# Identity products on TensorE between the adaLN dot products of a decoder layer

## The reference

```python
mod = (jax.nn.silu(c) @ w_ada[l] + b_ada[l]).reshape(b, N_MOD, D_MODEL)
sh1, sc1, g1 = mod[:, 0], mod[:, 1], mod[:, 2]
...
h = modulate(x, sh1, sc1)      # LayerNorm(x) * (1 + sc1) + sh1
y = swiglu(h, ffn1_w_gate[l], ffn1_w_up[l], ffn1_w_down[l])
x = layer_norm(ALPHA * x + 0.5 * g1[:, None, :] * y, ln1_g[l], ln1_b[l])
```

## Time and profile before

| | |
|---|---|
| median of the timed runs | 2340.41 us (3 runs, 2339.27 to 2340.97) |
| the profiled execution's own time | 2345.88 us |
| its span on the slowest core (core 5) | 2344.3 us |
| spans of the other cores | 2330.9 to 2340.4 us |
| PE busy on core 5 | 2258.2 us (96%) |
| DVE, ACT, POOL busy on core 5 | 1447.6, 765.0, 389.6 us |

### The profile page before, as it was taken

How to read it: one execution, slowest core, us unless ns; L and a number is a source line. 1 busy time by engine, 2 the same in 40 slices (tenths; PEclk the granted TensorE clock), 3 DMA queues, 4 the chain that set the end, 5 groups by cost and what they waited for, 6 DMA issues and landing times.

```text
span 2344.3 us, 41640 instructions; the slowest of 8 cores (2330.9 to 2344.3 us)
## 1 busy us (share of the span) xinstructions
PE 2258.2 (96%) x13832; PEld 1269.6 (54%) x13832; DVE 1447.6 (62%) x2928; ACT 765.0 (33%) x1554; POOL 389.6 (17%) x319
## 2 busy tenths in 40 slices
PE   1999999999999999999999999999999999999998
PEld 1554555555555556644555555555555555555555
DVE  5464465665564343378767676768585868676754
ACT  2521222222222232344343433434343343433321
POOL 0022321221110110013211111111111121211110
PEclk9899999999999999999999999999999999999999
DMA  9962879976563122043645464636464555554556
GB/s 310 312 226 102 163 196 210 199 189 162 180 211 97 71 80 83 1 171 109 238 175 204 161 218 149 224 145 225 153 215 163 202 177 198 180 191 169 208 183 239
DMA packets 123122, 415.48 MB, mean 177 GB/s; under 512 B 27296, under 2 KB 49568, under 8 KB 101408
## 3 DMA queue, kind: packets, MB, share of 16 engines
q1 hardware_dynamic: 87920, 396.92, 49.9%
q0 software_dynamic: 33696, 14.62, 5.3%
q10 hardware_dynamic: 1296, 1.29, 0.2%
HBM read 385.33 MB, written 56.10 MB: 188 GB/s over the span
## 4 chain that ended last, share of the span: by engine, by line
PE 88%; DVE 4%; DMA 3%; issue 2%; SPq 1%; POOL 1%; ACT 1%; DVEq 0%; POOLq 0%; ACTq 0%
PE ps L497 25%; PE ps L1237 24%; PE ps L1260 13%; PE ps L603 10%; PE ps L1046 3%; PE ps L1016 2%; PE ps L1164 2%; PE ps L1166 2%; PE ps L442 2%; PE ps L578 1%; SPq L367 1%; DMA t_arena<-ffn_w_down 1%; DMA t_arena<-w_ada_t 1%; PE ps L1135 1%; PE ps L1072 1%
## 5 line engine op out<-in xcount | busy, mean ns | idle before, releaser
L497 PE MATMUL ps<-t_arena 128*128 128x384 bf16 x3872 | 643.9, 329 | 20.5 <-ACT t_arena L424 17.3
L1237 PE MATMUL ps<-t_arena 128*128 128x384 bf16 (+1 forms) x3872 | 635.2, 322 | 1.2 <-DVE t_arena L426 1.2
L497 PEld LDWEIGHTS ps<-t_arena 128*128 128x128 bf16 x3872 | 381.2, 99 | 278.8 <-issue 29.4
L1237 PEld LDWEIGHTS ps<-t_arena 128*128 128x128 bf16 x3872 | 372.5, 98 | 243.8 <-issue 20.9
L392 POOL TENSOR_TENSOR t_stt<-t_stt,t_mhalf 128x1 f32<-128x1 f32 x193 | 120.5, 624 | 1436.3 <-DVE t_stt L391 1396.9
L399 ACT ACTIVATE t_arena<-t_arena,t_stt 128x1024 f32<-128x1024 f32 (+1 forms) x193 | 238.9, 1239 | 305.5 <-DVE t_stt L394 288.3
L488 DVE TENSOR_TENSOR t_arena<-ps,t_sg 128x384 bf16<-128x384 f32 x242 | 134.4, 556 | 318.6 <-PE ps L497 298.8
L1260 PE MATMUL ps<-t_arena 128*128 128x512 bf16 x1408 | 314.0, 379 | 1.7 <-DMA t_arena<-scr_d 1.7
L603 PE MATMUL ps<-t_arena 128*128 128x512 bf16 x1320 | 293.5, 382 | 4.7 <-DVE t_arena L550 4.7
L388 DVE BATCH_NORM_STATS2 t_stt<-t_arena 128x6 f32<-128x512 f32 x386 | 266.9, 692 | 41.2 <-DMA t_arena<-x_c 13.1
L527 POOL TENSOR_TENSOR t_arena<-t_arena 128x1024 f32<-128x1024 f32 x95 | 229.1, 2412 | 354.3 <-DVE t_arena L526 341.3
(11 more groups left out here) (90 smaller groups left out, 1524.4 us busy)
## 6 DMA issues: line engine op xcount, KB each, us to landing
t_arena<-scr_gu SPq DMA_DIRECT2D x121, 1024.0 KB, 6.6
t_arena<-scr_d SPq DMA_DIRECT2D x44, 1024.0 KB, 5.8
t_arena<-w_ada_t SPq DMA_DIRECT2D x72, 512.0 KB, 9.3
t_arena<-x_c SPq DMA_DIRECT2D x66, 512.0 KB, 5.4
t_arena<-scr_x SPq DMA_DIRECT2D x65, 512.0 KB, 6.6
t_arena<-ffn_w_gu SPq DMA_DIRECT2D x44, 512.0 KB, 10.8
t_arena<-ffn_w_down SPq DMA_DIRECT2D x44, 512.0 KB, 5.5
scr_x<-t_arena SPq DMA_DIRECT2D x33, 512.0 KB, 3.8
```

Source lines behind the costliest of these rows:

```text
L497: ins = e.matmul(bk.f[:, 0:T], lhsT=w.ap[:, kc, gu, s2 * 128:(s2 + 1) * 128], rhs=hT.ap[:, kc, 0:T], start=(kc == 0), stop=(kc == 7))
L1237: ins = e.matmul(bk.f[:, 0:T], lhsT=wv[:, kc, gu, s2 * 128:(s2 + 1) * 128], rhs=hTc.ap[:, kc, 0:T], start=(kc == 0), stop=(kc == 7))
```

## The change

A new generator `warm` issues n products of the 128 x 128 identity with itself into a PSUM bank of `FB`. It declares that it reads the buffer it is given, here `B_msc[1]`, so that it follows the last operation that wrote it. `ada_first` calls it after dots 9, 11 and 13 (60 products each), and after the last bias (40 products). The products' results are not used. Nothing else is edited; the line numbers behind the new code move by 10 to 14.

```diff
+        def warm(n, after_buf):
+            bk = yield from take(FB)
+
+            def mm(e, bk=bk):
+                for k in range(n):
+                    ins = e.matmul(bk.f[:, 0:128], lhsT=ident[:], rhs=ident[:], start=True, stop=True)
+                return ins
+            yield Op("pe", mm, [after_buf, B_const], [bk.buf], n * 0.06)
+            FB.give(bk)
+
         def ada_first():
             yield from until("csr0")
             for i in range(16):
@@
                 if i % 8 == 7:
                     yield mod_bias(i // 8, i // 8)
                     flags.add(("msc", i // 8))
+                if i in (9, 11, 13):
+                    yield from warm(60, B_msc[1])
+                elif i == 15:
+                    yield from warm(40, B_msc[1])
```

## The result

The changed kernel takes 1.0055 times the time of the kernel before (95% interval 1.0038 to 1.0072, seven runs of each; medians 2355.64 and 2340.83 us). Two of the seven runs of the change and one of the seven of before fell in a slower state of the chip; the ratio leaves them out, the medians count them. On the 2340.41 us of the runs shown that is +12.9 us, interval +8.9 to +16.9, or some 2353.3 us. I had forecast 2346.5 us, +6.1. The direction was right, the forecast size was half of the measured one.

A forecast was written before the change was run, and what follows sets the result against it. PE bounds the kernel behind 320 us, DVE's dots its start. Gate-up 15.8 us later, less give-backs, left +9.9, +7.8, +3.5 us on cores 0, 1, 5; taken as +6.1: 2346.5 us, range 2338 to 2354.

The forecast's parts named there:

- The dots wait: Before gate-up: dots 10, 12, 14 wait for bursts of 5.4, 5.0 and 5.0 us; gate-up starts 15.8 us later.
- The give-backs to the gate row: Up to the gate row: four terms leave +9.9, +7.8 and +3.5 us on cores 0, 1 and 5.
- the 1.0 us of clock that I left it: Behind the second tile's transposes: low clock after the new wait still costs 1.0 us.
- The new wait behind the transposes: After the second tile's transposes: PE idles 2.0 us for their evacuation, replacing the wait of about 3 us before them.
- It stays the shorter, so the 24 products that were moved are hidden in waits that PE had there: Gate row to down products: PE's 41.3 us stays below the multiplications' 44 to 46; uncovered, 24 products cost 3.9 us.
- last condition: Sign of being wrong: the stretch after the gate row takes up more than 3 us of the delay.
- The median's shift: Whole kernel: the median run moves by +6.1 us, to 2346.5 us.
- The last step, from three cores to the slowest of eight: End of the sum: between core 1 and core 5, the median's slowest core shifts 6.5 us, taken as 6.1.
- Only the first burst is cold: Rival, chance 0.24: the clock holds through the pauses, bursts take 11.9 us together, time 2342 us.
- Identity products don't raise the clock: Rival, chance 0.12: all bursts take 6.5 us, gate-up starts cold as before, time some 2354 us.
- Faster: Rival, chance 0.09: core 5's lost clock sets the time; short bursts and a shorter gate-row stretch give 2335 us.
- Refills of weights: Later weight loads: SP's refills wait some 10 us longer for casts but cost nothing; no gate-up product waits.

The follow-up runs named there:

- e1: The changed kernel with the same 220 products, but the bursts not declared as readers of the dots' buffer, so no dot waits: ratio 1.0003 to the kernel before.
- e2: The changed kernel with the bursts' estimated duration set to zero, giving the order of before while the dots' waits stay: ratio 1.0050 to the kernel before.
- e3: The changed kernel's order and waits, but each burst is one product instead of 60 or 40: ratio 1.0005 to the kernel before.
- e8: The changed kernel with its order kept and 120 products instead of 60 in the three bursts that dots wait for: ratio 1.0102 to the kernel before.
- e5: The changed kernel with its order kept and 30 products instead of 60 in the three bursts that dots wait for: ratio 1.0047 to the kernel before.
- e6: The changed kernel's order with no identity products and no waits for PE, made by longer estimated dots: ratio 0.9998 to the kernel before.
- e10: The changed kernel's order with no dot waiting, and e4's bursts of 60 and 16 products: ratio 0.9991 to the kernel before.
- e4: The changed kernel with no dot waiting and only 60 products after dot 13 and 16 after the bias: ratio 1.0006 to the kernel before.
- e7: e4 plus 36 identity products that wait for nothing, in PE's pause ahead of the second tile's transposes: ratio 0.9986 to the kernel before.
- e9: The kernel before plus only 36 identity products in PE's pause ahead of the second tile's transposes: ratio 1.0000 to the kernel before.
- e11: e7 run again on another chip: ratio 0.9971 to the kernel before.

## Why the prediction was right and where it was wrong

**The dots wait: right.** The bursts took 5.9, 4.8 and 4.0 us on the mean of the cores, 14.7 together, where I had 5.4, 5.0 and 5.0. Gate-up started 14.8 us later, where I had 15.8. The clock rose in the bursts, and fell in half of the pauses: of the sixteen bursts behind one, eight took 4.8 to 5.4 us, six took 3.51, and the third on cores 0 and 1 took 4.10 at a granted clock of 0.81. e1 and e2 show that the waits and not the products cost the time, e3 and e8 that the cost follows the bursts' length; e5 lies between them by its start, and nearer to the change than expected by its time.

**The give-backs to the gate row: right on the mean, wrong by core.** Of 14.8 us 7.6 were left at the gate row on the mean of eight; my three cores had 9.9, 7.8 and 3.5, a mean of 7.1. That the means agree is in part luck. Core 5 had +1.0 for my +3.5: its gate-up started 14.4 us later and not 15.8, and it didn't lose the 1.0 us of clock that I left it. Cores 0 and 1 had +15.7 and +13.7 for my +9.9 and +7.8, with a clock of 0.81 for a while, which I had not among my terms. The new wait behind the transposes was 1.9 to 2.2 us, predicted 2.0.

**"It stays the shorter, so the 24 products that were moved are hidden in waits that PE had there": this step failed.** I set the stretch behind the gate row at its old length and noted that uncovered the 24 products would cost 3.9 us. It grew from 43.7 to 46.8 us, 3.1 of these 3.9. I had set PE's path at 41.3 us of products, without the waits inside, and had read the room for them from core 5.

The waits have to be told apart. The last one, ahead of L578, was 2.5 us on the mean before (1.12 to 4.50) and is 1.0 us now, and 1.0 us stays even where the L488 waits only for PE. So 1.4 us of room was there, not 3.9. Core 5 had the most, and there the step held: its stretch went from 46.4 to 45.7 us. Cores 0 and 1 had shown a last wait of 1.12 us in my own rows, and grew by 2.1 and 2.7 us. The waits inside the stretch, for L488s that free PE's banks, grew from 2.4 to 3.6 us. Where PE waits there, the L488 stands behind pairs of multiplications on DVE. On core 5 of the changed kernel, DVE, then PE:

```profile
150.36 4.50 DVE L746 TENSOR_TENSOR t_arena<-t_arena 128x1024 bf16<-128x1024 f32 x2
154.78 1.01 DVE L488 TENSOR_TENSOR t_arena<-ps,t_sg 128x384 bf16<-128x384 f32 x2
```

```profile
155.47 20.96 PE L497 MATMUL ps<-t_arena 128*128 128x384 bf16 x128 [1.84 <-DVE t_arena L488]
```

With PE's busy time up by 3.4 us (38.8 to 42.2), these make the 3.1: +3.4, -1.4, +1.2, but for rounding. In the runs with the new order (e3, e5, e6, e8, e10) the stretch is 46.1 to 47.4 us and in those with the old order (e1, e2, e4, e7, e9, e11) 42.5 to 44.1. In the first the last L488 waits for PE on every core; in the second it stands behind a multiplication on every core, though not on every core does that hold it up. Why the waits inside grow with the order was not tested by a run of its own. The prediction named this stretch in its last condition (it "takes up more than 3 us of the delay"), with the other sign: it added 3.1.

**The median's shift.** With 3.1 us in place of nothing, my sum would have been 9.2 us, and inside the measured interval (+8.9 to +16.9), at its low end. My range (2338 to 2354 us) holds the measured 2353.3 us at its edge only, and its interval reaches beyond. The mean of the cores shows +10.7 at the down products and +12.2 at the end. The last step, from three cores to the slowest of eight, took 6.1 where my three cores had a mean of 7.1, because it leaned on core 5, for which the change was cheap; cores 0 to 4 and 6 lost 7.9 to 17.8 us at the down products. With 7.1 and the 3.1 us the sum is 10.2. In the profiled run the two longest cores, 2 and 3, also had a clock of 0.79 behind 2300 us, where core 5 before had 0.97. No experiment isolates that, and whether it is in the median run isn't known.

**The rivals.** *Only the first burst is cold* held for half of the sixteen later bursts (the second on cores 5 and 7, the third on the six others), on no core for both. *Identity products don't raise the clock* is refuted: on six of the eight cores one burst of 60 took 3.51 us, 58 ns a product, and core 5's gate-up started at full clock behind them. It came out near the measured time (2354) for a wrong reason. *Faster* forecast core 5's own gain, and its span is 5.1 us shorter, but not by that mechanism: its down products come 0.4 us later, the 5.4 us are gained behind them, and core 5 was no longer what sets the time.

**Refills of weights: right.** Core 3 of e2, 14 us late as well, has its 416 products in 67.76 us, as core 0 before, and core 5 of the changed kernel has its 376 in 61.26 us, 163 ns each: none waits for a cast.

## What to carry to other kernels

Warm TensorE with work that nothing waits for: a declared read of a buffer that is written again turns filler into a wait of the writer, and its price is the filler's length, while the same 220 products without it cost nothing that could be told. When products move from one side of a dependency to the other, compare the racing paths with their waits in them, wait by wait and on every core: only the part of the last wait that the other path causes is room, and the core with the most of it is the wrong one to read it from. And a gain of 2 us at a cold start was not seen in the time (e4, 1.0006); with the next pause filled as well it may be 3 to 7 us (e7, e11), at the edge of what these runs can tell.

## What the runs showed of the hardware

**Pauses of about 3 us let the clock fall on some cores only.** Behind pauses of 2.83 us the bursts of 60 took 3.51 to 5.41 us in one profile. Behind the 3.00 us pause the 24 transposes took over 2 us on three of eight cores before, on all eight in e1, on one in e2 and on five in e4. In e5, with bursts of 3.36 us between the same pauses, cores 5 and 7 stayed at 1.2 GHz through three bursts of 112 ns a product. Core 7's granted clock is 0.50 there, core 5's reads 1.00 at the same times, so at the start of a profile the record has to be checked against the durations. With 2.17 us of the 3.00 us pause filled (e7, e9, e11) the transposes took 1.50 us on all eight cores each time; e2 shows 1.50 us on seven without a fill, so these three runs are good evidence and no proof. The rule of the Trainium skill (TensorE: Matmul & The Clock Gate, HAM oscillation), that each group behind a wait starts cold, is told there of waits for DMAs that are mostly longer than these pauses; here it holds for eight of the sixteen bursts behind a pause.

**A third level, 0.81, in stretches.** Windows of 66 to 80 us of the changed kernel (length, PE busy, PEld, DVE, ACT, POOL busy, granted clock, DMA share, GB/s), first core 0, then core 5:

```profile
66.00:80.00 14.00, 14.00 (x73) 7.74 (x72) 8.68 (x21) 8.62 (x11) 2.00 (x3) 0.81 0.69 218
```

```profile
66.00:80.00 14.00, 12.96 (x96) 8.19 (x94) 10.02 (x26) 10.57 (x14) 2.00 (x3) 1.00 0.86 267
```

Core 0's 80 gate-up products took 15.91 us there, core 5's 13.16; the ratio is 0.83. Core 1 shows the same 0.81, cores 2 and 3 of the same die don't (0.97 and 1.00). In windows of 6 us cores 0 and 1 are at 0.81 or below from 69 to 105 us. The kernel before has such stretches too, on the other die. Windows of core 5, in the middle of products that never pause:

```profile
69.00:75.00 6.00, 6.00 (x30) 3.25 (x29) 2.92 (x6) 3.61 (x6) 0.00 (x0) 0.71 1.00 268
...
81.00:87.00 6.00, 6.00 (x32) 3.31 (x31) 2.32 (x4) 2.67 (x5) 0.00 (x0) 0.81 1.00 307
...
99.00:105.00 6.00, 6.00 (x36) 3.43 (x35) 2.75 (x5) 2.87 (x4) 0.00 (x0) 0.90 1.00 303
```

The first window is the low clock behind the pause, 1.7 us of loss (29% of 6). From 75 to 123 us the granted clock of the eight windows adds up to 3.0 us more (0.50 windows of 6 us), cores 4, 6 and 7 show dips in the same stretch (0.82 to 0.84 at 81 to 87 us), and cores 0 to 3 none. So of core 5's 4.4 us in its 416 products, all of which I had put down to the pause ahead, most was this level, which no filler in the pause takes away; that the changed kernel's profile has it on cores 0 and 1 and not on core 5 makes up part of the differences by core between the two profiles. The Trainium skill (TensorE: Matmul & The Clock Gate, section Seeing it yourself, on the peak-current limiter) gives 13/16 of the clock for a die on which three cores run dense matmuls, held while the load lasts. The level agrees. Its reach doesn't, for it is on two of a die's four cores here, and its duration doesn't, for behind 320 us the granted clock is 1.00 on core 5 under a load no less dense. Identity products aren't needed for such dips: e6 has none, and its cores 0 to 3 show 0.84 to 0.86 at 81 to 87 us. They go with the chip more than with the kernel. All four runs on one chip (e5 to e8) have them on cores 0 to 3 from 87 us on, and the seven runs on the two other chips show 1.00 there; cores 0 to 3 lost some 3 us to them in e7 and nothing in e11, which is the same kernel on another chip. What starts such a stretch no run here settles.
